# Starting the split-weight tiles of a two-block transformer kernel 64 bytes later in each partition

## Chip, cores and metric

The kernel is one program on one core of a Trainium2 chip. The metric is device microseconds of one execution, as the median of several runs.

## What is computed

Two blocks, each two layers deep, on 256 latent tokens and 256 context tokens of width 1024, all in fp32. The first block has a gated linear attention layer (GLA) and a state-space layer (SSD), each with a feed-forward net (FFN); the second block has two layers that mix neighbourhood, latent (MLA) and differential attention. Cut to what matters:

```python
def reference(x, c, ctx, ...):
    x = first_block(x, c, ctx, ...)    # i = 0: gla_mixer, i = 1: ssd_mixer; then layer_norm, FFN, layer_norm
    return second_block(x, c_2, ...)   # l = 0, 1: three attentions, merge_branches

def sq_relu_mlp(h, w1, w2):            # the FFN, 1024 -> 4096 -> 1024
    return jnp.square(jax.nn.relu(h @ w1)) @ w2

# every projection is h @ w: w_in, w_out, ffn_w1, ffn_w2, w_uq, w_ukv, w_br, ...
y = (sigmoid(g_na) * ((o_na * silu(z_na)) @ w_br[0]) + sigmoid(g_mla) * (...) + sigmoid(g_diff) * (...))
return y @ w_out
```

The context half is not needed in the last layer of either block, so some layers work on all 512 tokens and some on the 256 latent ones.

## The kernel before

**A projection.** Each weight matrix comes in slots of 128 x 1024 fp32 numbers (`SLOT`). SP loads a slot into one of four places of `wslots` (L194). ACT copies it, rounded, to `weights_hi` (L221), and DVE or POOL writes the difference to `weights_lo` (L231); both are rings of four slots, 4096 bytes each per partition. The input of the projection is split in the same way into `input_hi` and `input_lo` (or another pair of tiles, such as `ffn_hidden_hi` and `ffn_hidden_lo`). TensorE then makes three products for each 128 x 128 piece of weights: hi times hi, hi times lo, lo times hi, which together stand for one fp32 product.

**A matmul has two operands in SBUF.** One is loaded into the array first (128 columns, the rows of PEld in the profile), the other is then streamed through it (256 or 512 columns, the rows of PE). The trace names them in the order streamed, loaded: in `psum<-input_hi,weights_hi` the input is streamed and the weights are loaded. Each matmul here has a load of its own, and the load for the next matmul goes on while the present one streams. There are two arrangements (L239 to L255):

```python
def passes(self, n, cols, parts):              # weights loaded, input streamed
    ...
    out += [(hi[:, k, cols], xh), (hi[:, k, cols], xl), (lo[:, k, cols], xh)]
def passes_by_token(self, n, parts):           # input loaded, weights streamed
    ...
    out += [(xh, hi[:, k, :]), (xl, hi[:, k, :]), (xh, lo[:, k, :])]
```

The first is called feature-major below and is used for nearly everything; the second, token-major, makes the values of the attentions (`gla_v`, `na_v`, `diff_v`), and the products with `w_ukv` and `w_uq` in L3099 and L3083 stream their weights too. `product` (L278 to L289) issues the matmuls of a tile; L305, L322, L3588 and L3738 issue such products where other work runs beside them.

**Where the tiles lie.** A tile is placed in each partition behind the one that was declared before it, at a multiple of 32 bytes. Ahead of `wslots` lie 16,384 bytes of scratch and four constants of 32 bytes, so `wslots` starts at 128 modulo 512; it and the rings are 16,384 bytes long, so `weights_hi` and `weights_lo` start at 128 as well, and so does every 128-column piece in them, since pieces are 512 bytes apart. Then come `h1`, `h2`, the constant matrices, `cols`, `eps`, `mod1`, `mod2` and `lam`; behind `lam` lie the tiles of single stages. From the declared sizes these start, modulo 512, at:

| tile (streamed, or loaded where token-major) | used in | start modulo 512 |
|---|---|---|
| `input_hi`, `input_lo` of GLA | GLA | 0 |
| `gla_out_hi` / `gla_out_lo` | GLA's output projection | 0 / 96 |
| `input_hi`, `input_lo`, `ffn_hidden_hi`, `ffn_hidden_lo` of layer 0 | FFN 0 | 448 |
| `input_hi`, `input_lo` from the SSD layer on | SSD, FFN 1, block 2 | 320 |
| `ssd_out`, `ffn_hidden` of layer 1, `mix_o`, `merge_o`, `mla_cq`, `mla_ckv` (hi and lo) | SSD, FFN 1, block 2 | 320 |

Further rows (`k`) of these tiles are 1024 or 2048 bytes apart, and the latent half of a row starts 1024 bytes in, so that the value modulo 512 is the same for all of them. `eps` (two numbers for square roots, made once by POOL) and `lam` (the four numbers of the differential attention) are read in a few small instructions.

**The order of the work** is written out by hand, stage by stage, with semaphores; `make_plan` fixes the slots. Nothing in it looks at addresses. The function that the change touches follows, with what calls it.

Of the kernel before, what the change touches and what calls it, by code (L numbers as in the profile page):

```python
# [20 lines left out]
P = 128  # L21
# [9 lines left out]
DEPTH = 2  # L31
# [342 lines left out]
def build(nc, d, out, dump=None, until=99):  # L374
    ctx = ExitStack()
    with ctx:
        b = Build(nc, d, ctx)
        b.psum = ctx.enter_context(nc.psum_tensor("psum", [P, 8, 512], F32))
        b.wslots = b.sb(ctx, "wslots", [P, RAW, SLOT])
        b.whi = b.sb(ctx, "weights_hi", [P, RING, SLOT])  # L380
        b.wlo = b.sb(ctx, "weights_lo", [P, RING, SLOT])
        b.whi_r, b.wlo_r = b.whi[:].bitcast(F32R), b.wlo[:].bitcast(F32R)
        b.H1 = b.sb(ctx, "h1", [P, KD, T])
        b.H2 = b.sb(ctx, "h2", [P, KD, T])
        b.ident = b.sb(ctx, "ident", [P, P])
        b.snake = b.sb(ctx, "snake", [P, P])
        b.ones = b.sb(ctx, "ones", [P, P])
        b.half_ones = b.sb(ctx, "half_ones", [P, P])
        b.cols = b.sb(ctx, "cols", [P, 5, P])
        b.eps = b.sb(ctx, "eps", [P, 2])  # L390
        b.mod1 = b.sb(ctx, "mod1", [P, DEPTH, 48, 2])
        b.mod2 = b.sb(ctx, "mod2", [P, DEPTH, 24, 2])
        b.lam = b.sb(ctx, "lam", [P, DEPTH, 4])
        make_plan(b)
        with ExitStack() as early:
            b.ada_c = b.sb(early, "ada_c", [P, 2, KD, 32])
            b.ada_flat = b.sb(early, "ada_flat", [P, 512])
            b.ada_vec = b.sb(early, "ada_vec", [P, AM, 2])
            with b.joined():
                gla_layer(b)  # L400
                if until >= 3:
                    finish_layer(b, 0, ALL, None)
                if until >= 4:
                    ssd_layer(b)
        with ExitStack() as late:
            input_parts(b, late, False)
            if until >= 5:
                finish_layer(b, 1, LAT, b.H2)
            if until >= 6:
                with b.joined():  # L410
                    for l in range(DEPTH):
                        attention_layer(b, l, out)
        if until < 6:
            store_stage(b, b.H2 if until >= 5 else b.H1, out, dump)
# [442 lines left out]
def input_parts(b, st, raw=None):  # L857

    b.UH = b.sb(st, "input_hi", [P, KD, T])
    b.UL = b.sb(st, "input_lo", [P, KD, T])  # L860
    b.UH_r, b.UL_r = b.UH[:].bitcast(F32R), b.UL[:].bitcast(F32R)
    if raw is not False:
        b.raw = b.sb(st, "input_raw", [P, 2, T]) if raw is None else raw
# [535 lines left out]
def gla_layer(b):  # L1399
    st = ExitStack()  # L1400
    with st:
        qk = b.sb(st, "gla_qk", [P, GH, 2, T])
        v = b.sb(st, "gla_v", [P, TT, D])
        gate = b.sb(st, "gla_gate", [P, KD, T])
        cum = b.sb(st, "gla_cum", [P, 2, GH, T])
        qT, kT = qk[:, :, 0, :], qk[:, :, 1, :]
        stat = b.sb(st, "gla_stat", [P, GH, TT])
        oT = qk[:].rearrange("p h a t -> p (h a) t")
        room = [x[:].rearrange(s) for x, s in ((qk, "p h a t -> p (h a t)"), (v, "p t n -> p (t n)"),
                                               (gate, "p k t -> p (k t)"), (cum, "p z h t -> p (z h t)"))]  # L1410
        gla_project(b, qT, kT, v, gate, cum, room)
        at = b.nc.sbuf_base
        b.UH, b.UL = (b.nc.alloc_sbuf_tensor_at(f"gla_out_{x}", [P, KD, T], F32, offset=at + o) for x, o in (("hi", 4096), ("lo", OUT_LOW)))
        b.UH_r, b.UL_r = b.UH[:].bitcast(F32R), b.UL[:].bitcast(F32R)
        gla_core(b, qk, v, cum, oT, stat)
        gla_out(b, oT, gate, stat)
# [716 lines left out]
def ssd_layer(b):  # L2133
    st = ExitStack()
    with st:
        xs = b.sb(st, "ssd_x", [P, TT, SDI])
        bt = b.sb(st, "ssd_b", [P, NCTX // P, SG * SN])
        bT, cT = b.H2[:, :, NCTX:T], b.H1[:, :, 0:NCTX]
        z = b.sb(st, "ssd_z", [P, SDI // P, NLAT])
        y = xs[:, 0:2, :]  # L2140
        s = b.sb(st, "ssd_state", [P, 2, SDI])
        tok = b.sb(st, "ssd_tok", [P, 6, 2 * SH])
        dskip = b.sb(st, "ssd_dskip", [P, SH])
        rows = b.sb(st, "ssd_rows", [P, 3 * P])
        pick = b.sb(st, "ssd_pick", [P, 2 * SH])
        unit = b.sb(st, "ssd_unit", [P, P])
        hide = b.sb(st, "ssd_hide", [P, 2, P])
        ssd_project(b, xs, bt, bT, cT, z, s, tok, dskip, rows, pick, unit, hide)
        power = b.sb(st, "ssd_power", [P, 2, NLAT])
        ssd_core(b, xs, bt, bT, cT, y, z, s, tok, dskip, rows, pick, unit, hide, power)  # L2150
        ssd_out(b, y, s, power)
# [561 lines left out]
def attention_layer(b, l, out):  # L2713
    last = l == DEPTH - 1
    seg = LAT if last else ALL
    st = ExitStack()
    with st:
        o = b.sb(st, "att_o", [P, 3, BW // P, T])
        with ExitStack() as heads:
            qk = b.sb(heads, "att_qk", [P, 2 * BW // P, T])  # L2720
            m = {"q": qk[:, 0:BW // P], "k": qk[:, BW // P:], "v": b.sb(heads, "att_v", [P, TT, BW])}
            input_norm(b, l)
            project_heads(b, l, "na", seg, {**m, "z": o[:, 0]})
            with ExitStack() as latent:
                at = b.nc.sbuf_base
                n = {"q": qk, "k": b.sb(latent, "mla_k", [P, MLH, T]), "v": m["v"], "z": o[:, 1], "spare": o[:, 2, 0:2]}
                with ExitStack() as ranks:
                    size = QL // P * T
                    c = {"cq": [b.nc.alloc_sbuf_tensor_at(f"mla_cq_{x}_{l}", [P, QL // P, T], F32, offset=at + 4 * size * i)
                                for i, x in enumerate(("hi", "lo"))],  # L2730
                         "ckv": [b.sb(ranks, f"mla_ckv_{x}", [P, KVL // P, T]) for x in ("hi", "lo")],
                         "kr": o[0:MQK, 2, 2],
                         "rate": b.sb(ranks, "mla_token_rate", [P, 2, TT])}
                    with ExitStack() as fill:
                        attend_pairs(b, l, 0, {**m, "z": o[:, 0]}, last, LatentFill(b, fill, l, seg, c, o[:, 1]))
                    project_latent(b, l, seg, n, c)
                with ExitStack() as fill:
                    attend_pairs(b, l, 1, n, last, MixFill(b, fill, l, 0, seg, o))
            project_heads(b, l, "diff", seg, {**m, "z": o[:, 2]})
            with ExitStack() as fill:  # L2740
                attend_maps(b, l, {**m, "z": o[:, 2]}, last, MixFill(b, fill, l, 1, seg, o))
        merge(b, l, seg, o, out)
# [1553 lines left out]
```

How the kernel before makes its waits and increments, by code:

```python
    def load(self, sp, upto):  # L189
        for n in range(self.issued, min(upto + 1, len(self.slots))):
            src, kt, w, _ = self.slots[n]
            if n >= RAW:
                sp.wait_ge(*self.slot_free(n - RAW))
            sp.dma_start(self.slot(n), src.rearrange("(k p) w -> p k w", p=P))\
              .then_inc(self.tick(f"weights_in_{n % RAW}", 16), 16)
            self.issued = n + 1
# [15 lines left out]
    def round_weights(self, act, upto):  # L212
        upto = min(upto, len(self.slots) - 1)
        for n in range(self.next_split["act"], upto + 1):
            if self.slots[n][3]:
                if self.round_nth[n] > RING:
                    name, count = self.split_release[self.round_nth[n] - 1 - RING]
                    act.wait_ge(self.sem(name), count)
                act.wait_ge(*self.weights_in(n))
                act.activation(self.part(self.whi_r, n), self.slot(n), ACT.Copy)\
                    .then_inc(self.tick("weights_rounded"), 1)
        self.next_split["act"] = max(self.next_split["act"], upto + 1)
# [1 line left out]
    def split_weights(self, engine, name, upto):  # L225
        upto = min(upto, len(self.slots) - 1)
        for n in range(self.next_split[name], upto + 1):
            if self.slots[n][3] == name:
                engine.wait_ge(self.sem("weights_rounded"), self.round_nth[n])
                engine.tensor_tensor(self.part(self.wlo_r, n), self.slot(n), self.part(self.whi, n), ALU.subtract)\
                    .then_inc(self.tick(f"weights_split_{name}"), 1)
```

## Time and profile before

| | |
|---|---|
| median of 3 runs | 2462.53 us (2461.32 to 2464.13) |
| span of the profiled execution, first to last instruction | 2460.4 us |
| TensorE busy (PE) / its weight loads (PEld) | 96% / 79% of the span |
| DVE, ACT, POOL busy | 64%, 49%, 18% |
| mean granted TensorE clock | 0.984 |

The runs were timed without the profiler, and the profiled execution has no time of its own beside its span; the span is 2.1 us under the median. A busy share of TensorE says that matmuls follow each other without gaps; it does not say how long each one holds the array, since their ends overlap. For that, the rows below give the starts of matmuls in long unbroken stretches: the difference of two starts, by the number of matmuls between, is the pace of one.

### The profile page before, as it was taken

What the parts mean: (1) busy time and instruction counts of PE and PEld (TensorE: products, weight loads), DVE (VectorE), ACT (ScalarE), POOL (GpSimd) and SP (SyncE); (2) the same over time, 40 slices, a digit from 0 to 9 for tenths busy, and PEclk for the clock granted to TensorE, in tenths of its full rate; (3) what the DMA queues carried; (4) which work ended last, traced back from release to release, by engine and by line L of the source; (5) the groups of instructions that cost most, each with busy time, mean ns of one, the idle gap of its engine ahead of it and who ended that gap; (6) DMA issues with size and microseconds to landing.
All of it is one profiled execution on the core that took longest, in us unless ns stands there. A gap on an engine that the chain in (4) does not pass through costs nothing. (4 is left out here: it accounts for less than half of the span.)

```text
span 2460.4 us, 35031 instructions
## 1 busy us (share of the span) xinstructions
PE 2364.0 (96%) x13732; PEld 1940.8 (79%) x13732; DVE 1571.9 (64%) x2359; ACT 1217.7 (49%) x2090; POOL 450.9 (18%) x277
## 2 busy tenths in 40 slices
PE   7998999999999999999999999999999989989989
PEld 5776778887879888789998767677767878778878
DVE  5867978778765667687675454643566355564775
ACT  2666544223238334557454355763366243666364
POOL 0000000000017434000004431005211135404310
PEclk9999999999999999999999999999999999999999
DMA  8734427666535332446663231213222233334344
GB/s 316 213 118 149 152 78 210 185 187 187 157 102 138 95 92 62 137 138 179 183 179 96 73 95 54 69 44 91 69 69 78 77 97 106 100 92 120 84 112 129
DMA packets 416076, 302.13 MB, mean 123 GB/s; under 512 B 10210, under 2 KB 389192, under 8 KB 414888
## 3 DMA queue, kind: packets, MB, share of 16 engines
q1 hardware_dynamic: 414800, 299.45, 41.9%
q8 instruction: 110, 1.80, 0.3%
q10 hardware_dynamic: 1112, 0.44, 0.1%
q14 instruction: 54, 0.44, 0.1%
HBM read 298.80 MB, written 1.05 MB: 122 GB/s over the span
## 5 line engine op out<-in xcount | busy, mean ns | idle before, releaser
L221 ACT ACTIVATE weights_hi<-wslots 128x1024 fp32r<-128x1024 f32 (+1 forms) x408 | 427.1, 1051 | 251.7 <-PE psum L284 191.3
L284 PE MATMUL psum<-input_hi,weights_hi 128*128 128x512 f32 (+1 forms) x1384 | 494.1, 357 | 1.7 <-POOL weights_lo L231 0.7
L284 PE MATMUL psum<-input_hi,weights_lo 128*128 128x512 f32 (+1 forms) x1384 | 482.0, 348 | 0.0
L284 PE MATMUL psum<-input_lo,weights_hi 128*128 128x512 f32 (+1 forms) x1384 | 481.5, 348 | 0.0
L231 POOL TENSOR_TENSOR weights_lo<-wslots,weights_hi 128x1024 fp32r<-128x1024 f32 (+1 forms) x139 | 333.8, 2409 | 715.4 <-ACT weights_hi L221 714.7
L231 DVE TENSOR_TENSOR weights_lo<-wslots,weights_hi 128x1024 fp32r<-128x1024 f32 x269 | 330.8, 1239 | 159.8 <-ACT weights_hi L221 159.0
L284 PEld LDWEIGHTS psum<-input_hi,weights_hi 128*128 128x128 f32 x1384 | 261.3, 189 | 45.6 <-issue 8.8
L284 PEld LDWEIGHTS psum<-input_lo,weights_hi 128*128 128x128 f32 x1384 | 260.7, 188 | 38.0 <-issue 2.9
L284 PEld LDWEIGHTS psum<-input_hi,weights_lo 128*128 128x128 f32 x1384 | 260.5, 188 | 36.8
L284 PE MATMUL psum<-ffn_hidden_hi,weights_hi 128*128 128x512 f32 (+1 forms) x512 | 173.6, 339 | 0.0
L284 PE MATMUL psum<-ffn_hidden_hi,weights_lo 128*128 128x512 f32 (+1 forms) x512 | 172.5, 337 | 0.0
L284 PE MATMUL psum<-ffn_hidden_lo,weights_hi 128*128 128x512 f32 (+1 forms) x512 | 171.7, 335 | 0.0
L2851 DVE RECIPROCAL head_rstd<-head_rstd 128x512 f32<-128x512 f32 (+1 forms) x32 | 94.4, 2951 | 96.5 <-ACT head_rstd L2843 96.5
L3738 PE MATMUL psum<-input_hi,weights_hi 128*128 128x512 f32 (+1 forms) x384 | 134.6, 351 | 4.5 <-issue 3.3
L3738 PE MATMUL psum<-input_lo,weights_hi 128*128 128x512 f32 (+1 forms) x384 | 129.7, 338 | 0.0
L3738 PE MATMUL psum<-input_hi,weights_lo 128*128 128x512 f32 (+1 forms) x384 | 129.5, 337 | 0.0
L284 PEld LDWEIGHTS psum<-ffn_hidden_hi,weights_hi 128*128 128x128 f32 x512 | 96.8, 189 | 13.3 <-issue 3.6
L284 PEld LDWEIGHTS psum<-ffn_hidden_hi,weights_lo 128*128 128x128 f32 x512 | 96.5, 189 | 10.7
L284 PEld LDWEIGHTS psum<-ffn_hidden_lo,weights_hi 128*128 128x128 f32 x512 | 96.1, 188 | 10.8 <-issue 0.2
L1307 ACT ACTIVATE ffn_hidden<-psum 128x512 f32<-128x512 f32 (+1 forms) x64 | 31.4, 491 | 124.2 <-PE psum L284 117.1
L2325 DVE SCALAR_TENSOR_TENSOR ssd_conv<-psum,cols,ssd_conv 128x508 f32<-128x508 f32 (+3 forms) x128 | 87.3, 682 | 4.5
L3738 PEld LDWEIGHTS psum<-input_hi,weights_hi 128*128 128x128 f32 x384 | 72.8, 190 | 17.1 <-issue 7.9
(541 smaller groups left out, 4942.5 us busy)
## 6 DMA issues: line engine op xcount, KB each, us to landing
wslots<-w_in SPq DMA_DIRECT2D x132, 512.0 KB, 3.9
wslots<-ffn_w SPq DMA_DIRECT2D x128, 512.0 KB, 4.5
wslots<-ssd_w_in SPq DMA_DIRECT2D x49, 512.0 KB, 3.9
wslots<-ada_w SPq DMA_DIRECT2D x32, 512.0 KB, 4.5
h<-w_ada SPq DMA_DIRECT2D x28, 512.0 KB, 4.3
wslots<-gla_w_in SPq DMA_DIRECT2D x25, 512.0 KB, 5.0
input_raw<-ada_w SPq DMA_DIRECT2D x24, 512.0 KB, 4.0
ada_slab<-ada_w SPq DMA_DIRECT2D x24, 512.0 KB, 3.9
```

Of the source, the lines that this page charges most:

```text
L221: act.activation(self.part(self.whi_r, n), self.slot(n), ACT.Copy)\
L231: engine.tensor_tensor(self.part(self.wlo_r, n), self.slot(n), self.part(self.whi, n), ALU.subtract)\
L284: ins = pe.matmul(out_of(self.bank(g)), l, r, start=first and i == 0, stop=last and i == len(pairs) - 1, skip_group_check=not (first and l ...
L1307: act.activation(hid[:, j % NH, :], b.bank(g)[:, a:e], ACT.Relu).then_inc(b.reads_out(g), 1)
L2325: ins = dve.scalar_tensor_tensor(dst[:, :, o], src[:, :, i], tap(k), dst[:, :, o], ALU.mult, ALU.add)
L2851: dve.reciprocal(r, r).then_inc(b.tick("dve_step"), 1)
L3738: ins = pe.matmul(b.bank(g)[:, a:e], w, u, start=x == 0, stop=x == len(pairs) - 1, skip_group_check=True)
```

## The change

Two declarations move: `eps` (8 bytes, padded to 32) and `lam` (32 bytes) are declared right behind `wslots`.

```diff
         b.wslots = b.sb(ctx, "wslots", [P, RAW, SLOT])
+        b.eps = b.sb(ctx, "eps", [P, 2])
+        b.lam = b.sb(ctx, "lam", [P, DEPTH, 4])
         b.whi = b.sb(ctx, "weights_hi", [P, RING, SLOT])
         b.wlo = b.sb(ctx, "weights_lo", [P, RING, SLOT])
...
         b.cols = b.sb(ctx, "cols", [P, 5, P])
-        b.eps = b.sb(ctx, "eps", [P, 2])
         b.mod1 = b.sb(ctx, "mod1", [P, DEPTH, 48, 2])
         b.mod2 = b.sb(ctx, "mod2", [P, DEPTH, 24, 2])
-        b.lam = b.sb(ctx, "lam", [P, DEPTH, 4])
```

`weights_hi` and `weights_lo` then start at 192 modulo 512, and so do `h1`, `h2`, `ident`, `snake`, `ones`, `half_ones` and `cols`, which lie between; `mod1` and `mod2` move by 32 bytes. `wslots` stays at 128, and everything behind `lam` (the tiles of the table) stays where it was. No instruction is added, removed or reordered on any engine; only addresses differ.

## Rows read from the trace of the kernel before

**Rows 1.** The page: head, busy time by engine, TensorE's granted clock.
```profile
span 2460.4 us, 35031 instructions
PE 2364.0 (96%) x13732; PEld 1940.8 (79%) x13732; DVE 1571.9 (64%) x2359; ACT 1217.7 (49%) x2090; POOL 450.9 (18%) x277
...
PEclk9999999999999999999999999999999999999999
```
**Rows 2.** Stretches (us): length, PE, PEld, DVE, ACT, POOL busy, clock, DMA share, GB/s.
```profile
350.00:720.00 370.00, 368.32 (x1634) 294.61 (x1633) 278.17 (x311) 127.01 (x181) 8.21 (x11) 0.99 0.56 167
...
1333.00:2000.00 667.00, 654.82 (x3228) 501.20 (x3229) 341.12 (x644) 331.02 (x563) 154.63 (x93) 0.99 0.27 75
2000.00:2460.00 460.00, 428.69 (x2890) 364.58 (x2888) 275.83 (x466) 250.19 (x409) 138.66 (x90) 0.98 0.38 104
```
**Rows 3.** FFN 0, timeline of PE (start, us each): first and last of 72 matmuls.
```profile
439.62 0.39 PE L284 MATMUL psum<-input_hi,weights_lo 128*128 128x512 f32 x1
...
455.88 0.39 PE L284 MATMUL psum<-ffn_hidden_lo,weights_hi 128*128 128x512 f32 x1
```
**Rows 4.** Block 2, feature-major, timeline: first and last of 70.
```profile
1949.78 0.39 PE L305 MATMUL psum<-input_hi,weights_hi 128*128 128x512 f32 x1
...
1965.88 0.40 PE L305 MATMUL psum<-input_hi,weights_hi 128*128 128x512 f32 x1
```
**Rows 5.** Block 2, token-major, timeline: first and last of 23.
```profile
2053.11 0.39 PE L284 MATMUL psum<-weights_hi,input_lo 128*128 128x512 f32 x1
...
2058.16 0.39 PE L284 MATMUL psum<-weights_lo,input_hi 128*128 128x512 f32 x1
```
**Rows 6.** GLA, feature-major, timeline: first and last of 70.
```profile
69.69 0.39 PE L284 MATMUL psum<-input_lo,weights_hi 128*128 128x512 f32 x1
...
85.78 0.40 PE L284 MATMUL psum<-input_lo,weights_hi 128*128 128x512 f32 x1
```
**Rows 7.** GLA, token-major, timeline: first and last of 62.
```profile
175.79 0.39 PE L284 MATMUL psum<-weights_hi,input_hi 128*128 128x512 f32 x1
...
189.97 0.39 PE L284 MATMUL psum<-weights_hi,input_lo 128*128 128x512 f32 x1
```
**Rows 8.** Last token-major matmul at 1390.26 us and its neighbour: mean ns.
```profile
L284 PE MATMUL psum<-weights_lo,input_hi 128*128 128x512 f32 x1 | 0.4, 397 | 0.0
L284 PE MATMUL psum<-weights_hi,input_lo 128*128 128x512 f32 x1 | 0.4, 388 | 0.0
```
**Rows 9.** FFN 0, two of its matmul groups: count, busy us, mean ns.
```profile
L284 PE MATMUL psum<-input_hi,weights_hi 128*128 128x512 f32 x232 | 91.4, 394 | 0.0
...
L284 PE MATMUL psum<-input_lo,weights_hi 128*128 128x512 f32 x232 | 90.5, 390 | 0.0
```
**Rows 10.** Before FFN 1's down products, 256 columns, timeline: first and last of 117.
```profile
1143.81 0.28 PE L284 MATMUL psum<-input_hi,weights_lo 128*128 128x256 f32 x1
...
1156.96 0.28 PE L284 MATMUL psum<-input_lo,weights_hi 128*128 128x256 f32 x1
```
**Rows 11.** 256 columns, the largest matmul group of the whole span.
```profile
L284 PE MATMUL psum<-input_hi,weights_hi 128*128 128x256 f32 x552 | 156.7, 284 | 1.3 <-POOL weights_lo L231 0.7 <-PEq L1044 0.6
```
**Rows 12.** FFN 1, 256 columns, timeline: first and last of 138.
```profile
1179.79 0.28 PE L284 MATMUL psum<-ffn_hidden_hi,weights_hi 128*128 128x256 f32 x1
...
1195.93 0.28 PE L284 MATMUL psum<-ffn_hidden_hi,weights_lo 128*128 128x256 f32 x1
```
**Rows 13.** Stretches of 256 columns at the slower pace: busy time by engine.
```profile
1160.00:1300.00 140.00, 140.00 (x1189) 139.94 (x1188) 96.33 (x136) 70.69 (x107) 5.29 (x2) 1.00 0.63 180
1076.00:1107.00 31.00, 31.00 (x266) 31.00 (x265) 23.04 (x40) 14.54 (x19) 0.00 (x0) 1.00 0.67 186
```
**Rows 14.** FFN 0, the lines of DVE and ACT that split the weights.
```profile
L231 DVE TENSOR_TENSOR weights_lo<-wslots,weights_hi 128x1024 fp32r<-128x1024 f32 x61 | 73.8, 1219 | 7.8 <-ACT weights_hi L221 7.8
L221 ACT ACTIVATE weights_hi<-wslots 128x1024 fp32r<-128x1024 f32 x63 | 66.5, 1056 | 106.9 <-PE psum L284 106.9
```

## The prediction

> **What bounds the kernel now.** I began with the page. TensorE is busy 96% of the span and its clock stands at the full 2.4 GHz nearly throughout (PEclk 9 in each slice); DVE, at 64%, is next [rows 1]. By stretch it is tighter still: PE is busy for 368.3 of 370 us in FFN 0, and for 654.8 and 428.7 of 667 and 460 in block 2's two layers [rows 2]. In such stretches no wait ends anything. The end is set by how fast one matmul follows another, so I read the timeline for that: two starts far apart, divided by the steps between them. FFN 0 gives 16.26 us over 71 steps, 229.0 ns for 512 columns [rows 3]. Block 2 gives 16.10 over 69, 233.3 ns [rows 4]. Both stretches stream 512 columns and load 128, at the full clock, without a gap, and yet differ by 1.9%. Over some 4,000 matmuls that is more than most waits here are worth.
>
> **What the pace goes with.** Engines, shapes and clock are alike in both, but the starts of the operands are not. Call the distance the start of the streamed tile less the start of the loaded one. In FFN 0 it is 448 - 128 = 320; in block 2 it is 320 - 128 = 192. The token-major matmuls turn the operands round: 128 - 320 = -192, which is 320 modulo 512. They lie in the same stage as the 233.3 ns, and they take 5.05 us over 22 steps, 229.5 ns, as FFN 0 does [rows 5]. GLA's feature-major products have 0 - 128, which is 384, and run at 16.09 over 69, 233.2 ns [rows 6]; its token-major ones have 128 - 0 = 128 and run at 14.18 over 61, 232.5 ns [rows 7]. So 320 is the fast distance, and 128, 192 and 384 are slow, all within 0.8 ns. That 128 and 384 agree suggests that only the value modulo 256 counts; I use that where I say so.
>
> **The change part by part.** No instruction comes, goes or moves. The cost is that the distances change: 64 less where weights are loaded, 64 more where they are streamed. Counts are make_plan's slots by 24 matmuls.
>
> FFN 0, 64 slots, 1536 matmuls, 320 to 256. No long stretch shows 256. Modulo 256 it is 0, and the trace has distance 0 only where stages meet: the last token-major matmul streams `weights_lo` (128) while `weights_hi` (128) is loaded for the next. That one is held for 397 ns where its neighbour takes 388 [rows 8]; the five such places in the trace all read 397 or 398. FFN 0's groups lie between 390 and 394 [rows 9]. So I put 256 with the slow distances, at 233.3: 4.3 ns by 1536 is +6.6 us. Bounds: from below twice the fastest pace for 256 columns, 2 x 113.4 = 226.8 [rows 10], -3.4 us; from above FFN 0's matmul of about 392 ns [rows 9] lengthened to 397, 5 ns, +7.7 us. It is one matmul's evidence against an unknown, so the lower end stays open.
>
> Block 2 and part of the SSD layer, 512 columns feature-major, 111 slots, 2664 matmuls, 192 to 128: from 233.3 to between 232.5 [rows 7] and 233.2 [rows 6]. I take 0.4 ns, -1.0 us; ends -2.1 and -0.3.
>
> Token-major in block 2, 480 matmuls, 320 to 384: from 229.5 to 233.2 as GLA's [rows 6], +1.8 us; with 108 of 384 columns (three quarters of that each) +0.3. Ends 0 and +2.5.
>
> GLA feature-major, 408 matmuls, 384 to 320: from 233.2 to 229.0, -1.6 us. GLA token-major, 192 matmuls, 128 to 192: +0.2. GLA's output projection, 192 matmuls whose low half starts at 96: 0, ends 0.8 either way.
>
> 256 columns, all feature-major at 320, 177 slots, 4248 matmuls (552 of them are the largest group [rows 11]), 192 to 128. Here the distance does not settle the pace: 16.14 us over 137 steps, 117.8 ns, in FFN 1 [rows 12], and 13.15 over 116, 113.4 ns, some 35 us earlier [rows 10], from the same starts. Which pace a stretch falls into is decided at its start and then held: 140 us and 31 us run at the slower throughout, 1189 and 266 matmuls [rows 13]. At 512 columns 128 and 192 are alike, so I leave this mix as it is: 0. Ends: those 1455 slow ones all become fast, -6.4 us (4.4 ns each); the other 2793 all become slow, +12.3 us.
>
> The other engines: ACT's rounding (1056 ns) and the subtraction (1219 ns) now read and write at other starts, as do the users of `h1`, `h2`, `cols`, `eps` and `lam` [rows 14]. A slot is used for 24 matmuls, 5.5 us; were both to take 10% longer, they would be hidden behind it. Without that cover the two together are 2.3 us a slot. Loads into `h1` and `h2` are hidden as well, so 0.
>
> Sum: 6.6 - 1.0 + 1.8 + 0.3 - 1.6 + 0.2 = **+6.3 us**, one for one, since PE is without gaps where the large terms lie. On the span of 2460.4 us that gives 2466.7; the median of the runs stands 2.1 us above the span, so 2468.8.
>
> **A rule that speaks against all this.** The rows say that two operands in SBUF disturb each other by 4.3 ns a matmul, as their starts lie. The Trainium skill, "TensorE: Matmul & The Clock Gate", says in "Step-by-step: what each phase is for" that TensorE reads SBUF through two independent ports, one for each operand, and in "Back-to-back issue gap" that a warm matmul follows after N / 2.4 + 2.5 ns. By that the pace would be 215.8 ns for 512 columns wherever tiles lie, and the change would do nothing. The trace does not agree: 229.0 and 233.3.
>
> **The rivals.**
> - *Starts do not matter* (the pace goes with the stage or with how a stretch begins). For it: two paces from the same starts at 256 columns. Against it: 229.5 and 233.3 side by side in one stage, sorted by arrangement [rows 4, 5]. The time is 2462.5, and a partial cancelling lands here too (256 columns gain 6.4 while FFN 0 loses 6.6). 0.25 together.
> - *Faster: the stretches of 256 columns settle at 113.4 ns, and FFN 0 stays at 229.0.* Price -6.4; with the small terms (-1.0 + 1.8 + 0.3 - 1.6 + 0.2 = -0.3) it gives 2455.8. It decides if FFN 0's pace stays below about 230 ns: each nanosecond there costs 1.5 us. For it: the faster pace is common already, and the slow one is held for one long stretch by chance of its start. Against it: the 397 ns at distance 0 [rows 8]. 0.27.
> - *Slower still: 256 columns all at 117.8 ns.* 6.3 + 12.3 gives 2481.1. For it, distance 128 has shown no fast pace at 512 columns. Against it, 192 has not either, and yet is fast at 256. 0.08.
>
> The tiles do start where the change says, as their declared sizes decide, so I leave out that rival.
>
> **How the numbers follow.** About 0.2%, 4.9 us, is what a measurement of this kernel tells from no change. My forecast has 0.40, so slower has 0.40 + 0.08 = 0.48, same 0.25, faster 0.27. The range runs from 2453 (the faster rival with FFN 0 at 227) to 2479 (the forecast with most of the 256-column bound). If slower is right, its own range is 2467.5 to 2481.
>
> **What would show it.** In FFN 0 of the changed profile, 72 matmuls should span about 16.57 us rather than 16.26, and mean durations should rise from 390 to 394 ns to about 395 and more. Token-major products in block 2 should go to 233 and GLA's feature-major ones to 229. In 1160 to 1300 us the count of matmuls tells the two paces: 1189 is the slower one, some 1235 the faster. The prediction is wrong if FFN 0 stays at 229 or drops, or if these stretches change pace as a whole.

## The result, and the profile after

The changed kernel takes 2472.68 us (median of 4 runs, 2467.42 to 2475.22) against 2463.33 us of the kernel before (4 runs, 2461.32 to 2464.55). The ratio is 1.0036, with a 95% interval of 1.0024 to 1.0047: slower by 5.9 to 11.6 us. The forecast was 2468.8.

The page of the changed kernel, head and busy times; they answer to [rows 1]:

```profile
span 2471.3 us, 35031 instructions
## 1 busy us (share of the span) xinstructions
PE 2376.0 (96%) x13732; PEld 1960.2 (79%) x13732; DVE 1571.0 (64%) x2359; ACT 1217.8 (49%) x2090; POOL 450.1 (18%) x277
```

The profiled execution's own time is 2473.08 us. The span grew by 10.9 us and TensorE's busy time by 12.0, while DVE, ACT and POOL stayed within 0.9 us. So the difference lies on TensorE. How much of it is the pace of matmuls is summed up below.

The changed kernel's stretches (us; length, PE, PEld, DVE, ACT, POOL busy with counts, clock, DMA share, GB/s), against [rows 2, 13]:

```profile
350.00:720.00 370.00, 367.80 (x1652) 296.87 (x1650) 277.55 (x312) 127.72 (x182) 8.22 (x11) 0.99 0.56 167
1160.00:1300.00 140.00, 140.00 (x1169) 139.90 (x1168) 94.05 (x137) 70.05 (x107) 0.73 (x1) 1.00 0.62 181
1076.00:1107.00 31.00, 31.00 (x264) 31.00 (x263) 23.23 (x40) 13.85 (x18) 0.00 (x0) 1.00 0.67 185
```

Two things stand in these counts. In FFN 0, more matmuls fit into 370 us (1652, before 1634), so FFN 0 became *faster*. (A count is of matmuls that touch the stretch.) In FFN 1's 140 us of 256 columns, fewer fit (1169, before 1189, which was already the slower of the two paces known), and 264 for 266 in the 31 us.

For the paces I read PE's timeline of the changed kernel as in [rows 3 to 7]: the first and last of an unbroken row of matmuls (start, us each). FFN 0, 76 matmuls, 17.00 us over 75 steps, 226.7 ns (229.0 before, [rows 3]):

```profile
439.82 0.39 PE L284 MATMUL psum<-input_hi,weights_hi 128*128 128x512 f32 x1
...
456.82 0.39 PE L284 MATMUL psum<-ffn_hidden_hi,weights_hi 128*128 128x512 f32 x1
```

Block 2, feature-major, 72 matmuls, 16.50 over 71, 232.4 ns (233.3 before, [rows 4]):

```profile
1949.78 0.40 PE L3738 MATMUL psum<-input_hi,weights_lo 128*128 128x512 f32 x1
...
1966.28 0.40 PE L305 MATMUL psum<-input_lo,weights_hi 128*128 128x512 f32 x1
```

GLA, feature-major, 76 matmuls, 17.16 over 75, 228.8 ns (233.2 before, [rows 6]):

```profile
68.76 0.39 PE L284 MATMUL psum<-input_hi,weights_hi 128*128 128x512 f32 x1
...
85.92 0.39 PE L284 MATMUL psum<-input_hi,weights_hi 128*128 128x512 f32 x1
```

The groups of the changed kernel say the same in the mean duration of one: FFN 0's first group is at 392 ns (394 in [rows 9]), and the largest group of 256 columns at 288 (284 in [rows 11]):

```profile
L284 PE MATMUL psum<-input_hi,weights_hi 128*128 128x512 f32 x232 | 90.9, 392 | 0.0
```
```profile
L284 PE MATMUL psum<-input_hi,weights_hi 128*128 128x256 f32 x552 | 158.9, 288 | 1.1 <-PEq L1044 0.6 <-POOL weights_lo L231 0.5
```

Averaged over all matmuls of a kind that follow each other without a gap in the two traces, and multiplied by the counts of the prediction:

| kind | distance modulo 512 | ns before | ns after | us |
|---|---|---|---|---|
| 256 columns, 4248 | 192 to 128 | 115.6 | 119.0 | +14.4 |
| FFN 0, 1536 | 320 to 256 | 229.0 | 227.1 | -2.9 |
| 512 columns feature-major, 2664 | 192 to 128 | 233.3 | 232.7 | -1.6 |
| block 2 token-major, 480 (and 108 of 384 columns) | 320 to 384 | 229.3 (173.3) | 232.7 (175.9) | +1.6 (+0.3) |
| GLA feature-major and output projection, 600 | 384 to 320 (the output's low half 480 to 416) | 232.3 | 229.4 | -1.7 |
| GLA token-major, 192 | 128 to 192 | 232.4 | 233.3 | +0.2 |

The sum is +10.3 us, of the span's 10.9. The agreement is a little closer than the parts are. Both traces hold the same matmuls in the same order, so each interval between neighbouring starts can be set against its counterpart. Those of matmuls that follow each other without a gap, at the clock's higher level (2.4 GHz), give +9.8 us. Those that touch the lower level (1.2 GHz) in one trace or the other give +4.1, and all the rest, at gaps and among small matmuls, -3.1. One place shows the share of the clock: what the kernel before does from 1302 to 1333 us, behind FFN 1, takes 2.9 us longer in the changed kernel, at a granted clock of 0.80 against 0.89; in the kernel below that undoes the change in FFN 0 alone, and has the distances of the change here, it takes 0.3 us longer, at 0.89.

### The profile page after: what moved, and what is told of

It reads as the page before. It is cut to its first block and busy times, and to the rows that moved or that the text cites. A ratio compares the mean times of both kernels' runs of the same rounds, so it can differ in the third digit from the quotient of the medians.

```text
span 2471.3 us, 35031 instructions
## 1 busy us (share of the span) xinstructions
PE 2376.0 (96%) x13732; PEld 1960.2 (79%) x13732; DVE 1571.0 (64%) x2359; ACT 1217.8 (49%) x2090; POOL 450.1 (18%) x277
```

## The experiments

The theory is that the pace is set by the distance modulo 256 between the start of the streamed tile and that of the loaded one, and by nothing else of the change. The rivals are that the weights' own start counts, that the stage counts, or that distance 0 is slow, as I had forecast.

### All tiles moved together

```diff
         b.wslots = b.sb(ctx, "wslots", [P, RAW, SLOT])
+        b.eps = b.sb(ctx, "eps", [P, 2])
+        b.lam = b.sb(ctx, "lam", [P, DEPTH, 4])
...
-        b.eps = b.sb(ctx, "eps", [P, 2])
...
-        b.lam = b.sb(ctx, "lam", [P, DEPTH, 4])
+        b.sb(ctx, "pad", [P, 16])
...
-        ss = b.sb(st, "diff_ss", [P, len(groups), DFH])
+        ss = b.cols[:, 4, 64:64 + len(groups) * DFH].rearrange("p (g h) -> p g h", h=DFH)
```

> The weights start at 192 modulo 512 as in the change, but the 64 bytes that left their old place are filled by an empty tile, so every tile behind moves by 64 as well and every distance (streamed start less loaded start) is as in the kernel before; the sums of squares of the differential attention (64 bytes) lie in an unused part of cols to make room. Theory (the distance counts): the time of before, 2463 us within 3; FFN 0 at 229.0 ns, 256 columns between 113 and 118 ns. Rival (the weights' own start counts): the time of the change, about 2472.7 us, with 227.1 ns in FFN 0 and 119.0 ns at 256 columns.

Measured: 2462.77 us, ratio to before 1.0004 (0.9995 to 1.0013). FFN 0 in its timeline, 76 matmuls, 17.16 over 75, 228.8 ns, as before:

```profile
439.73 0.39 PE L284 MATMUL psum<-input_lo,weights_hi 128*128 128x512 f32 x1
...
456.89 0.39 PE L284 MATMUL psum<-ffn_hidden_lo,weights_hi 128*128 128x512 f32 x1
```

256 columns average 115.9 ns. The weights start where the change puts them and the time is that of before: the loss goes with the distances, not with the place of the weights, of `h1`, `h2` or of `cols`.

### The weights at 0, and at 64, modulo 512

The first of these two moves `mod2` ahead of the weights, the second `mod2`, `eps` and `lam`.

```diff
         b.wslots = b.sb(ctx, "wslots", [P, RAW, SLOT])
+        b.mod2 = b.sb(ctx, "mod2", [P, DEPTH, 24, 2])
...
-        b.mod2 = b.sb(ctx, "mod2", [P, DEPTH, 24, 2])
```
```diff
         b.wslots = b.sb(ctx, "wslots", [P, RAW, SLOT])
+        b.mod2 = b.sb(ctx, "mod2", [P, DEPTH, 24, 2])
+        b.eps = b.sb(ctx, "eps", [P, 2])
+        b.lam = b.sb(ctx, "lam", [P, DEPTH, 4])
...
-        b.eps = b.sb(ctx, "eps", [P, 2])
...
-        b.mod2 = b.sb(ctx, "mod2", [P, DEPTH, 24, 2])
-        b.lam = b.sb(ctx, "lam", [P, DEPTH, 4])
```

> mod2 (384 bytes) stands right behind wslots, the weights start at 0 modulo 512. Distances modulo 256: 64 for block 2 feature-major and all 256 columns, 192 for FFN 0 and token-major, 0 for GLA. Theory (the distance modulo 256 sets the pace, in whichever stage it occurs): block 2 at 229.0 ns (2664 matmuls by -4.3 = -11.5 us), FFN 0 at 233.3 (+6.6), token-major at 233.3 (+1.8), GLA at 227.1 (408 by -6.1 and 192 by -5.4 = -3.5); together -6.6, and 256 columns anything from 113.4 ns (-9.3) to as before (115.6): 2447 to 2457 us. Rival (the stage or the weights' start sets it): FFN 0 stays at 229 or below and block 2 at 233, time 2463.

> mod2, eps and lam stand right behind wslots, the weights start at 64 modulo 512. Distances modulo 256: 0 for block 2 feature-major, token-major and all 256 columns, 128 for FFN 0, 192 for GLA feature-major. Theory (distance 0 modulo 256 is the fastest, as FFN 0 showed after the change): block 2 at 227.1 ns (2664 by -6.2 = -16.5 us), token-major at 227.1 (-1.1), FFN 0 at 232.5 (+5.4), GLA about 0; together -12.2, and 256 columns from 113.4 ns (-9.3) to 115.6: 2441 to 2451 us. Rival (as in my prediction, distance 0 is slow, and FFN 0 gained by something else): block 2 stays at 233 or rises, time 2463 to 2470.

Measured: 2462.95 us with the weights at 0 (ratio 1.0004, 0.9990 to 1.0017) and 2469.35 with them at 64 (1.0028, 1.0017 to 1.0040). Both times miss what I expected and lie where the rivals put them, so the paces have to decide. Over long rows those at 512 columns are as the theory has them. (Averaged over all of block 2's feature-major matmuls, short rows too, distance 0 gives 228.2 ns rather than 227.1.) Timeline of the kernel with the weights at 0: FFN 0, 75 matmuls, 17.27 over 74, 233.4 ns; block 2, 74 matmuls, 16.71 over 73, 228.9 ns. The two stages have changed places:

```profile
439.65 0.39 PE L284 MATMUL psum<-input_hi,weights_hi 128*128 128x512 f32 x1
...
456.92 0.39 PE L284 MATMUL psum<-ffn_hidden_hi,weights_lo 128*128 128x512 f32 x1
```
```profile
1949.74 0.39 PE L305 MATMUL psum<-input_hi,weights_hi 128*128 128x512 f32 x1
...
1966.45 0.39 PE L284 MATMUL psum<-input_lo,weights_hi 128*128 128x512 f32 x1
```

Timeline of the kernel with the weights at 64: block 2 at distance 0 modulo 256, 74 matmuls, 16.54 over 73, 226.6 ns:

```profile
1949.78 0.39 PE L3738 MATMUL psum<-input_lo,weights_hi 128*128 128x512 f32 x1
...
1966.32 0.39 PE L305 MATMUL psum<-input_hi,weights_lo 128*128 128x512 f32 x1
```

What I got wrong is 256 columns. I had let them range from 113.4 ns to 115.6 ns, as if no distance could be worse than that of before. They average 117.2 ns with the weights at 0 (4248 by +1.6 = +6.8 us, which takes back the -6.6) and 119.8 ns with them at 64 (+17.8 us, against -12.2). For later comparison, the stretch from 1175 to 1235 us, in FFN 1; first the kernel before, then the change, then the weights at 64:

```profile
1175.00:1235.00 60.00, 60.00 (x512) 60.00 (x511) 40.08 (x57) 29.01 (x44) 0.00 (x0) 1.00 0.66 187
```
```profile
1175.00:1235.00 60.00, 60.00 (x502) 60.00 (x501) 37.52 (x49) 26.95 (x39) 0.00 (x0) 1.00 0.66 188
```
```profile
1175.00:1235.00 60.00, 60.00 (x502) 60.00 (x502) 36.73 (x45) 26.28 (x36) 0.00 (x0) 1.00 0.64 183
```

A matmul lasts 0.28 us in the profile, so those that overlap the edges count too; 60.28 us over 512 is 117.7 ns, over 502 it is 120.1 ns.

The 117.2 ns at distance 64 is an average of two paces, and they are the two of distance 192 [rows 10, 12]. With the weights at 0, FFN 1 runs at 117.8 ns, but the row behind FFN 0, 311 matmuls, takes 35.13 us over 310 steps, 113.3 ns (timeline):

```profile
752.63 0.28 PE L284 MATMUL psum<-input_lo,weights_hi 128*128 128x256 f32 x1
...
787.76 0.28 PE L284 MATMUL psum<-input_hi,weights_lo 128*128 128x256 f32 x1
```

### FFN 0 by itself

Three kernels move FFN 0's tiles alone: on top of the weights at 64 (128 bytes), on the kernel before (192 bytes), and on the change (64 bytes, which undoes its effect there). They differ in this line, with `[P, 32]`, `[P, 48]` and `[P, 16]`:

```diff
         if second:
+            b.sb(st, "pad", [P, 48])
             input_parts(b, st)
```

> As the run with the weights at 64, and 128 bytes of padding ahead of FFN 0's input tiles, so that FFN 0 is at distance 0 as well. Theory: FFN 0 at 227.1 ns instead of 232.5, 1536 matmuls, -8.3 us against the run with the weights at 64, so 2433 to 2443 us, the best of all. Rival (distance 0 is slow): FFN 0 at 233 or above, no gain over that run.

> The kernel before with 192 bytes of padding ahead of FFN 0's input tiles: FFN 0 goes from distance 320 to 0 modulo 512 (0 modulo 256, as in the change), nothing else moves. Theory (distance 0 modulo 256 is the fastest at 512 columns): 227.1 instead of 229.0 ns for 1536 matmuls, -2.9 us, about 2460.3. Rival (the term as I predicted it, 233.3 ns): +6.6 us, about 2470.

> The change with 64 bytes of padding ahead of FFN 0's input tiles: FFN 0 is back at distance 320, all else as changed. Theory: the change loses the one part that gained, +2.9 us against the change, about 2475.5, all of it at 256 columns (119.0 ns) and in small terms. Rival (FFN 0 is what slows the change): the time of before, 2463.

Measured, in this order: 2462.16 us, 7.2 below the kernel with the weights at 64, measured beside it (expected -8.3; the ratios to before are 0.9998, 0.9988 to 1.0007, and 1.0028); 2458.32 us (ratio 0.9985, 0.9976 to 0.9993, a gain of 1.7 to 5.9 us); 2473.64 us (1.0043, 1.0029 to 1.0057). The first time lies far above the 2433 to 2443 expected, since 256 columns average 119.8 ns there too. The last shows the loss without the part that gained; that it is above the change's 1.0036 has the expected sign, but the intervals overlap. Timelines of FFN 0 in the first and in the second, 77 matmuls each, 17.22 and 17.23 over 76, 226.6 and 226.7 ns:

```profile
439.73 0.39 PE L284 MATMUL psum<-input_hi,weights_lo 128*128 128x512 f32 x1
...
456.95 0.39 PE L284 MATMUL psum<-ffn_hidden_hi,weights_hi 128*128 128x512 f32 x1
```
```profile
439.76 0.39 PE L284 MATMUL psum<-input_hi,weights_lo 128*128 128x512 f32 x1
...
456.99 0.39 PE L284 MATMUL psum<-ffn_hidden_hi,weights_hi 128*128 128x512 f32 x1
```

So distance 0 is the fastest seen so far at 512 columns, and a +6.6 us for FFN 0 is excluded.

### Half the step: 32 bytes

One kernel moves `eps` alone ahead of the weights; the other pads 32 bytes behind `lam`.

```diff
         b.wslots = b.sb(ctx, "wslots", [P, RAW, SLOT])
+        b.eps = b.sb(ctx, "eps", [P, 2])
...
-        b.eps = b.sb(ctx, "eps", [P, 2])
```
```diff
         b.lam = b.sb(ctx, "lam", [P, DEPTH, 4])
+        b.sb(ctx, "pad", [P, 8])
```

> Half of the change: only eps (32 bytes) moves ahead of the split weights, which start at 160. Distances modulo 256: 160 for block 2 feature-major and all 256 columns, 32 for FFN 0, 96 for token-major. Theory, if the pace moves gradually with the distance: FFN 0 about 228.0 ns (-1.5 us), block 2 233.0 (-0.8), token-major 230.8 (+0.9), 256 columns 117.3 ns (4248 by +1.7 = +7.2); about 2468.8. Rival (only steps of 64 bytes count): each pace is that of the neighbour below or above, FFN 0 at 227.1 or 229.0 and 256 columns at 115.6 or 119.0, so 2460 or 2475.

> The kernel before with 32 bytes of padding behind lam: the weights stay, everything behind moves by 32. Distances modulo 256: 224 for block 2 feature-major and all 256 columns, 96 for FFN 0, 32 for token-major, 160 for GLA. Theory, if the pace moves gradually: block 2 between 233.3 and 227.1, so 230.2 (2664 by -3.1 = -8.3 us), FFN 0 230.8 (+2.7), token-major 228 (-0.5), 256 columns between 115.6 and 119.8 ns, so 117.7 (+8.9): about 2466, ends 2455 and 2475. If 224 is better than 192 at 256 columns too (below 115.6 ns), it is 2457 or less and points to a faster kernel.

Measured: 2478.23 us (1.0062, 1.0048 to 1.0076) and 2478.59 us (1.0063, 1.0049 to 1.0076). Neither guess held: half of the change costs more than all of it. Every odd multiple of 32 is slow at 512 columns. FFN 0 at distance 32 (first kernel, 75 matmuls, 17.27 over 74, 233.4 ns) and at 96 (second, 74 matmuls, 17.03 over 73, 233.3 ns):

```profile
439.68 0.40 PE L284 MATMUL psum<-input_hi,weights_lo 128*128 128x512 f32 x1
...
456.95 0.40 PE L284 MATMUL psum<-ffn_hidden_lo,weights_hi 128*128 128x512 f32 x1
```
```profile
439.81 0.39 PE L284 MATMUL psum<-input_hi,weights_hi 128*128 128x512 f32 x1
...
456.84 0.40 PE L284 MATMUL psum<-ffn_hidden_lo,weights_hi 128*128 128x512 f32 x1
```

With the other runs this gives the pace for all eight distances, averaged over the gapless matmuls of a trace:

| distance modulo 256 | 0 | 32 | 64 | 96 | 128 | 160 | 192 | 224 |
|---|---|---|---|---|---|---|---|---|
| 512 columns, ns | 227.1 | 233.3 | 229.0 | 233.3 | 232.7 | 234.2 | 233.3 | 233.1 |
| 256 columns, ns | 119.8 | not tried | 117.2 | not tried | 119.0 | 117.9 | 115.6 | 118.3 |

By these averages distance 192, that of the kernel before, is the best of the six at 256 columns and among the slow ones at 512; 0 is the other way round. No single place of the weights serves both. The averages at 256 columns hide that most of these distances show more than one pace over long rows: 113.3 and 117.8 ns at 192 and at 64, 117.3 and 118.7 at 160, 118.6 and 120.0 at 128. So 192 and 64 differ in how many rows fell into the slower pace, and 64 was profiled in one execution; that 192 is better than 64 is not shown.

### A version that beats both kernels

Wide tiles that belong to one stage can be moved by themselves: 512 columns to distance 0, 256 columns left at 192.

```diff
         if second:
+            b.sb(st, "pad", [P, 48])
             input_parts(b, st)
...
+        b.sb(st, "pad", [P, 32])
         input_parts(b, st)
...
-        b.sb(st, "inputs_room", [P, 488])
+        b.sb(st, "inputs_room", [P, 520])
...
+        if l == 0:
+            b.sb(st, "pad", [P, 16])
         self.oh = b.sb(st, "mix_o_hi", [P, BW // P, T])
...
+        if l == 0:
+            b.sb(st, "pad", [P, 16])
         oh = b.sb(st, "merge_o_hi", [P, BW // P, T])
```

(The sums of squares move as in the first experiment.)

> The kernel before with every stage's own wide (512-column) tiles moved to distance 0 modulo 256, and the 256-column ones left at 192: 192 bytes of padding ahead of FFN 0's input tiles, 128 ahead of GLA's (and of the room kept for them), 64 ahead of mix_o and merge_o in block 2's first layer; the sums of squares of the differential attention lie in an unused part of cols to make room. Theory: FFN 0 -2.9 us (227.1 instead of 229.0 ns), GLA's feature-major 400 matmuls by -5.3 ns = -2.1, its token-major 190 by -5.3 = -1.0, 296 of mix_o and merge_o by -6.2 = -1.8; together -7.8, about 2455. Rival: the parts outside FFN 0 lie beside waits and give nothing, 2459 as FFN 0 alone.

Measured: 2457.65 us against 2463.58, ratio 0.9972 (0.9962 to 0.9982), a gain of 4.4 to 9.4 us. GLA's timeline, 77 matmuls, 17.23 over 76, 226.7 ns, where it was 233.2 [rows 6]:

```profile
68.67 0.39 PE L284 MATMUL psum<-input_hi,weights_lo 128*128 128x512 f32 x1
...
85.90 0.39 PE L284 MATMUL psum<-input_hi,weights_hi 128*128 128x512 f32 x1
```

It beats both kernels. The intervals of this version and of FFN 0 alone overlap, so the share of GLA and `mix_o` is shown by their paces and not by the time.

### What sets the pace within a stretch of 256 columns

The two paces at one distance [rows 10, 12] were still open. In the kernel before, the faster one ends at one place: where a single plain fp32 product with `ones`, for the context's norm, comes in between. Timeline of the kernel before:

```profile
1159.11 0.28 PE L284 MATMUL psum<-input_hi,weights_lo 128*128 128x256 f32 x1
1159.22 0.59 PE L1246 MATMUL psum<-context_rate,ones 128*128 128x256 f32 x2
1159.47 0.47 PE L284 MATMUL psum<-input_hi,weights_hi 128*128 128x256 f32 x1
1159.77 0.28 PE L284 MATMUL psum<-input_lo,weights_hi 128*128 128x256 f32 x1
```

Ahead of it matmuls follow at 113.4 ns, behind it at 117.8, to the end of FFN 1. The profiles of three other kernels at distance 192, all tiles moved together, FFN 0 alone and the version above, turn at the same product. Two kernels change the interruption, on top of the version above:

```diff
                             pe.wait_ge(b.sem("norm_added"), b.nth("norm_added", KD))
+                            pe.matmul(b.psum[:, 7, 0:NCTX], b.ones[:], context_rate[:], start=True, stop=True)
                             pe.matmul(b.psum[:, 7, 0:NCTX], b.ones[:], context_rate[:], start=True, stop=True)\
                                 .then_inc(b.tick("square_added"), 1)
```
```diff
-                            pe.matmul(b.psum[:, 7, 0:NCTX], b.ones[:], context_rate[:], start=True, stop=True)\
+                            pe.matmul(b.psum[:, 7, 0:NCTX], b.ones[:], context_rate[:], start=True, stop=True)
+                            pe.matmul(b.psum[:, 7, 0:8], b.ones[:], context_rate[:, 0:8], start=True, stop=True)\
                                 .then_inc(b.tick("square_added"), 1)
```

> As the run with all wide tiles at 0, and the one plain fp32 product of context_rate with ones in FFN 1 (L1246 of the kernel before), after which every profile at distance 192 went from 113.4 to 117.8 ns, is issued twice in a row with the same result. It costs about 0.3 us. Theory (a stretch of 256 columns keeps the pace it restarts with, and a longer or shorter interruption restarts it elsewhere): if the second product restarts it at 113.4, the 140 us behind it hold some 1230 matmuls instead of 1189, and the time falls by up to 1170 x 4.4 ns = 5 us, to about 2453. Rival (any such product leaves it at 117.8, or the pace there goes with the tile): 1185 to 1190 in 1160 to 1300 us, and the time of the run with all wide tiles at 0, 2458.

> As the run with all wide tiles at 0, and behind the same product its first 8 columns once more (same values), which shifts the restart by a small and odd amount. Theory as in the run with the product twice: 113.4 ns and up to -5 us if it restarts at the faster pace; if both runs stay at 117.8 ns, the restart is not what decides, or both land on the slower pace. Rival: 1185 to 1190 matmuls in 1160 to 1300 us and 2458 us.

Measured: 2454.14 us with the product twice (0.9959, 0.9948 to 0.9971, single runs from 2447.02 to 2458.72) and 2457.29 us with eight columns more (0.9974, 0.9965 to 0.9983). The stretch from 1175 to 1235 us, first with the product twice, then with eight columns more:

```profile
1175.00:1235.00 60.00, 60.00 (x532) 60.00 (x531) 43.28 (x65) 32.78 (x53) 0.00 (x0) 1.00 0.68 193
```
```profile
1175.00:1235.00 60.00, 60.00 (x512) 60.00 (x511) 40.95 (x59) 30.63 (x48) 0.00 (x0) 1.00 0.64 182
```

With the product twice, 532 matmuls fit where 512 did: 113.3 ns from the same tiles at the same distances. I had named counts for 1160 to 1300 us; in both kernels that stretch holds a gap (PE busy 137.5 and 138.1 us), so I read the shorter one. This fits a pace that is chosen where a stretch restarts and held until the next interruption. That the second product chose it rests on one execution against the four that turned, and paces also differ between these kernels where nothing near was edited: a row of 239 matmuls that begins with `merge_o`, near 2400 us, runs at 113.4 ns in the version above and at 117.8 in both kernels built on it. A later product of the same form agrees: in FFN 1's last down products (timeline of the kernel with the product twice),

```profile
1256.07 0.28 PE L284 MATMUL psum<-ffn_hidden_hi,weights_lo 128*128 128x256 f32 x1
1256.18 0.59 PE L941 MATMUL psum<-h,ones 128*128 128x256 f32 x2
1256.42 0.47 PE L284 MATMUL psum<-ffn_hidden_hi,weights_hi 128*128 128x256 f32 x1
```

the pace turns from 113.4 to 117.8 ns at it. In the kernel with eight columns more it turns from 117.8 to 113.4 at the same product, and in the kernel before it stays at 117.8 across it. An interruption may thus turn the pace either way or leave it.

Single runs with the product twice spread over 11.7 us, against 6.4 in the version above and 7.4 with eight columns more, but also 11.4 with the weights at 0, where no product was doubled. That would fit a restart that falls either way from run to run, but one execution of each was profiled, and the granted clock is a rival: the four shortest of the ten runs (2447.02 to 2450.08 us) have a mean of 0.985 to 0.987, the six others (2453.74 to 2458.72) one of 0.981 to 0.984. Of the 11.1 us between the two profiled spans, 2447.1 with the product twice and 2458.2 in the version above, FFN 1's long row of 911 matmuls makes 4.0; the mean clock of the two is 0.986 and 0.983. The interval overlaps that of the version above. That the second product is a lasting gain is not shown.

## Why the prediction was right, and where it was wrong

**Sign and range.** Slower was the likeliest case at 0.48, and 2472.68 lies in the whole range (2453 to 2479) and in that of the slower case (2467.5 to 2481). In part this is luck: both signs came that the prediction had named against itself, that "FFN 0 stays at 229 or drops" and that the stretches of 256 columns "change pace as a whole". Its two largest terms were wrong, in opposite directions, and partly cancelled. What held in every run is the reading beneath the terms: in the long stretches TensorE is without gaps, the other engines do not matter (ACT's rounding averages 1058 ns in FFN 0 after the change, 1056 in [rows 14]), and the pace goes with the distance between the operands' starts, modulo 256 (at 256 columns with where a row restarts as well). The rival that starts do not matter is excluded by the tiles moved together (1.0004) beside the change (1.0036).

**FFN 0: the step that failed.** "So I put 256 with the slow distances, at 233.3" gave +6.6 us; it measured 227.1 ns, -2.9 us, near the lower end of -3.4, and the runs show distance 0 to be the fastest of eight. The evidence was one matmul's duration of 397 ns where the arrangement turns round [rows 8]. A duration is not a pace, since the profile's matmul ends are modelled. Nor was the 397 ns the price of distance 0. In the trace of before, 31 of block 2's 480 token-major matmuls last 397 or 398 ns, and only four of them stand where the arrangement turns; the others stream and load at distance 64. In the changed kernel the same two tiles, `weights_lo` streamed and `weights_hi` loaded for the next, have moved together and are at distance 0 still, and there the same matmul lasts 390 ns and its neighbour 398 (group lines at 1398.47 us):

```profile
L284 PE MATMUL psum<-weights_hi,input_lo 128*128 128x512 f32 x1 | 0.4, 398 | 0.0
L284 PE MATMUL psum<-weights_lo,input_hi 128*128 128x512 f32 x1 | 0.4, 390 | 0.0
```

At four of the five such places it is now 390 to 392. The faster rival had this part right ("FFN 0's pace stays below about 230 ns").

**256 columns: the term that was mis-sized.** "At 512 columns 128 and 192 are alike, so I leave this mix as it is: 0" measured +14.4 us, and passed even the bound of +12.3, since 118.6 to 120.0 ns is beyond the slower pace of 117.8 that I took for an end. The bound itself was too wide: the average before, 115.6 ns, lies midway between 113.4 and 117.8, so that about half of the 4248 were slow already, not 1455, and all at 117.8 would have been about +9.3 us. The order of the distances at 512 columns does not carry over to 256: there 192 has the lowest average of those tried and 128 is among the worst. The rival "slower still", at 0.08, came nearest: it had all of these matmuls slow, though at the known slower pace, not at a third one, and its +12.3 nearly sizes the term. Its time of 2481.1 was too high because of FFN 0's +6.6 in it. The two errors are 9.5 us too much and 14.4 too little, so that the time came out closer than its terms.

**The small terms** held: 512 columns feature-major -1.6 (forecast -1.0, ends -2.1 and -0.3), token-major +1.6 (+1.8) and +0.3 (+0.3), GLA -1.7 (-1.6) and +0.2 (+0.2).

**The signs I had named.** 72 matmuls in FFN 0 were to take 16.57 us instead of 16.26; at 226.7 ns they take 16.10. GLA at 229 (228.8) came as named; token-major in block 2 averages 232.7 for a forecast of 233. For 1160 to 1300 us I had named 1189 or 1235; it was 1169, a third pace.

**The rule weighed against the rows.** No distance brought a wide matmul below 226.6 ns. The Trainium skill, "TensorE: Matmul & The Clock Gate", section "Back-to-back issue gap", gives N / 2.4 + 2.5 ns, which is 215.8 ns for 512 columns, and names no place of the tiles. The traces of the change and of the eleven experiments do not agree, and between them the matmuls of FFN 0 move by 6.7 ns with the starts alone. The same section calls its formula the gap of an isolated matmul, which the prediction passed over, and puts a stream of loads and matmuls of 512 columns at about 131 ns; no row here comes near that either.

**What stays open.** Why the pace goes with the distance, and why 256 and 512 columns rank the distances differently, was not settled: no run separates the load that precedes a matmul from the one that goes on beside it. Nor does any run show what makes a restart choose one of two paces.

## What to carry to other kernels

Where TensorE is busy without gaps, read the pace of matmuls over long rows of starts, sort it by columns and by the distance between the streamed and the loaded tile modulo 256, and treat each number of columns as a table of its own; the best distance for one may be the worst for another. A few bytes of padding ahead of one stage's tiles are then worth a try (here 0 for 512 columns; 192, by its average, for 256; and at 512 no odd multiple of 32), while tiles that all stages share should be moved only after summing both. One matmul at a hand-over is no evidence for the pace of thousands, and the slowest pace seen is no upper bound for an arrangement that has not been seen.

## What the runs showed of the hardware

- With shapes, engines and order alike, at the clock's higher level, matmuls of 512 columns follow each other every 226.6 to 234.2 ns over long rows and those of 256 columns every 113.3 to 120.1 ns, by the distance of the operands' starts modulo 256. The kernel's time moves from 2458 (FFN 0 alone) to 2479 us (the tail 32 bytes later) by padding alone.
- At 256 columns one distance can show two paces, each held over a long row: 113.3 and 117.8 ns at 192 and at 64, 118.6 and 120.0 ns at 128. What chooses between them was not shown.
- At 256 columns and distance 192, the pace turned from 113.4 to 117.8 ns at one plain fp32 product in between, for the next 140 us. In the one profiled execution with a second such product behind it, 113.3 ns followed.
